# A token's two slots sorted by round, slot tables made with the rows as the stationary operand, and the last quad's second adds issued round by round

## The reference

```python
pg = softmax(t @ rg_w + rg_b);  pg_top, g_idx = top_k(pg, 1)        # one of 4 groups
le_sel = (t @ re_w + re_b).reshape(-1, 4, 4)[group of the token]
e_val, e_idx = top_k(le_sel, 2)                                     # two of its 4 experts
wts = softmax(e_val) * pg_top
y = hres + sum over the two experts of wts * ((silu(t @ w1) * (t @ w3)) @ w2)
```

## Time and profile before

| | us |
|---|---|
| median of 3 runs | 840.67 (837.34 to 842.12) |
| the profiled execution, its own time | 839.54 |
| its span in the trace | 837.7 |
| PE busy | 795.4 (95%) |
| DVE, ACT, POOL busy | 384.5, 225.9, 278.6 |

### The profile page before, as it was taken

One profiled execution on the slowest core, in us unless ns is written; L12 is line 12 of the kernel. 1 busy time (PEld: TensorE's weight loads), 2 busy tenths in 40 slices (PEclk: granted clock), 3 DMA queues, 4 the chain that ended last, 5 costly groups with the idle time before them and its releaser, 6 DMA issues.

```text
span 837.7 us, 14312 instructions
## 1 busy us (share of the span) xinstructions
PE 795.4 (95%) x5314; PEld 566.5 (68%) x5314; DVE 384.5 (46%) x700; ACT 225.9 (27%) x427; POOL 278.6 (33%) x204
## 2 busy tenths in 40 slices
PE   9999999989999998999999999999999789999991
PEld 8887777666677786777776777788888544333330
DVE  4671676757478589555551311543311632020210
ACT  4122324331423634114313222422201512020110
POOL 0000421244654773335453545523000021342223
PEclk9999999999999999999999999999999979999996
DMA  9243632245555531345453541161156769999943
GB/s 369 91 145 93 211 101 77 76 143 159 170 182 178 166 120 63 91 143 166 145 164 114 166 163 64 63 215 65 51 202 251 297 228 377 391 378 386 371 148 48
DMA packets 72154, 147.23 MB, mean 176 GB/s; under 512 B 13207, under 2 KB 47016, under 8 KB 70036
## 3 DMA queue, kind: packets, MB, share of 16 engines
q1 hardware_dynamic: 65716, 135.43, 46.0%
q0 software_dynamic: 5920, 10.82, 5.2%
q10 hardware_dynamic: 448, 0.06, 0.1%
HBM read 137.71 MB, written 18.90 MB: 187 GB/s over the span
## 4 chain that ended last, share of the span: by engine, by line
PE 85%; DVE 8%; ACT 2%; DMA 2%; issue 1%; POOLq 0%; POOL 0%; SPq 0%; DVEq 0%; ACTq 0%
PE ps L854 21%; PE ps L578 13%; PE ps L1157 10%; PE ps L1061 7%; PE ps L823 7%; PE ps L1226 5%; PE ps L621 3%; PE ps L593 3%; PE ps L876 2%; PE ps L923 2%; PE ps L653 2%; PE ps L567 1%; PE ps L1146 1%; DMA tmp<-in_xT 1%; PE ps L709 1%
## 5 line engine op out<-in xcount | busy, mean ns | idle before, releaser
L578 PE MATMUL ps<-xn,ring 128*128 128x268 f32 (+1 forms) x576 | 138.4, 395 | 1.0 <-ACT qb L1319 0.9
L578 PEld LDWEIGHTS ps<-xn,ring 128*128 128x128 f32 x576 | 108.2, 192 | 26.1 <-issue 3.4
L2415 POOL TENSOR_TENSOR kv<-kv,sgd 128x1024 f32<-128x1024 f32 (+1 forms) x32 | 79.9, 2510 | 120.0 <-DVE tmp L1760 70.3
L1462 ACT ACTIVATE sgt<-sgt,vec 128x260 f32<-128x260 f32 x60 | 30.2, 511 | 143.5 <-DVE sgt L2022 79.3
L823 PE MATMUL ps<-br,ring 128*128 128x260 f32 x256 | 61.7, 388 | 2.1 <-DVE sgt L2026 1.3
L2505 POOL DMA_INDIRECT out_y<-cst,gtab x24 | 37.3, 1555 | 76.4 <-DVE cst L2340 35.7
L854 PE MATMUL ps<-xn,ring 128*128 128x260 f32 x240 | 58.8, 388 | 2.3 <-ACT cst L1319 1.3
L854 PE MATMUL ps<-xn,qb 128*128 128x260 f32 x240 | 57.7, 383 | 0.0
L1061 PE MATMUL ps<-qk,ring 128*128 128x260 f32 x256 | 56.5, 383 | 0.0
L823 PEld LDWEIGHTS ps<-br,ring 128*128 128x128 f32 x256 | 47.6, 190 | 12.9 <-issue 2.8
L1061 PEld LDWEIGHTS ps<-qk,ring 128*128 128x128 f32 x256 | 48.6, 190 | 7.8 <-issue 0.4
(11 more groups left out here) (474 smaller groups left out, 1468.4 us busy)
## 6 DMA issues: line engine op xcount, KB each, us to landing
ring<-in_w_mg SPq DMA_DIRECT2D x32, 640.0 KB, 4.3
kv<-in_kc SPq DMA_DIRECT2D x128, 128.0 KB, 2.1
kv<-in_vc SPq DMA_DIRECT2D x128, 128.0 KB, 2.1
ring<-in_w_in SPq DMA_DIRECT2D x24, 512.0 KB, 4.7
kv<-in_w SPq DMA_DIRECT2D x8, 1024.0 KB, 15.0
br<-in_w SPq DMA_DIRECT2D x7, 1024.0 KB, 14.8
sgd<-in_w SPq DMA_DIRECT2D x6, 1024.0 KB, 16.4
qk<-in_w SPq DMA_DIRECT2D x6, 1024.0 KB, 12.2
```

What stands on the lines that cost most here:

```text
L578: mm = pe.matmul(ps[:, 2 * (t % 2) + h, 0:hw], wsl(c, k), xnv[:, k, col0 + h * hw:col0 + (h + 1) * hw], start=(k == 0), stop=(k == KT - 1))
L1462: act.activation(g, g, ACT.Sigmoid, bias=vv(V_BM + 8 * "ABCD".index(n) + m + i)).then_inc(g_a, 1)
L2415: pool.tensor_tensor(kb, kb, qbc[:, b:b + 1, :].to_broadcast([P, HALF // 2 + (half and u), 256]), ALU.mult)\
```

## The change

The positions of a token's two slots are sorted (`slot_f`: five minima, then five maxima), so kind 0 is the slot with the smaller position ("early") and kind 1 the other ("late"). The table matmuls have `oh_row` as the stationary operand and `marks` as the moving one, so that the result comes with slots on partitions and tiles on columns; it needs no transpose. Three are issued for each block: both kinds into one bank (the sum) and the late kind alone into another. The softmax weights are exchanged where the first choice is not the early one, and their table has two matmuls for each block. All `hTr` transposes are between the ranks and the table. `oh_row` of the first two blocks is made ahead of `marks`. In the last quad POOL issues the late adds of round r as soon as early adds of rounds up to r and late adds of the rounds before have landed.

```diff
-            rows_of(hTr, 0, NB)
 
             pe.wait_ge(sel_ok, 1)
...
-            for b in range(1, 3):
+            for b in range(NB):
                 rows_of(hTr, b, NB + b)
+
+            def by_rows(bk, j, b, mark, first, last):
+                return pe.matmul(ps[:, bk, 0:n_t], oh_row[0:RB, NB * j + b, :], marks[0:RB, mark, b, :], start=first, stop=last)
+
             for b in range(NB):
-                pe.wait_ge(oh_ok, 2 * b + 3)
+                pe.wait_ge(oh_ok, max(5, 2 * b + 3))
                 for j in range(2):
-                    mm = pe.matmul(ps[32 * j:32 * j + n_t, 5, 0:P], marks[0:RB, j, b, :], oh_row[0:RB, NB * j + b, :],
-                                   start=(b == 0), stop=(b == NB - 1), tile_position=(0, 32 * j))
+                    by_rows(4, j, b, j, b + j == 0, b + j == NB)
+                mm = by_rows(5, 1, b, 1, b == 0, b == NB - 1)
             mm.then_inc(tab_t[0], 1)
-            pe.wait_ge(sel_ok, 2)
-            pe.transpose(ps[:, 5, P:P + 64], slots[0:64], ident[0:64, 0:64]).then_inc(tab_tt[0], 1)
-            rows_of(hTr, 3, NB + 3)
-            rows_of(hTr, 4, NB + 4)
             pe.wait_ge(oh_ok, 2 * NB + 2)
-            pe.wait_ge(tt_a, NB + 3)
+            pe.wait_ge(tt_a, 2 * NB)
             for b in range(NB):
                 for j in range(2):
-                    mm = pe.matmul(ps[32 * j:32 * j + n_t, 2, 0:P], marks[0:RB, 2 + j, b, :], oh_row[0:RB, NB * j + b, :], ...
+                    mm = by_rows(7, j, b, 2 + j, b + j == 0, b + j == NB)
             mm.then_inc(wts_t[0], 1)
-            pe.wait_ge(sel_ok, 3)
-            pe.transpose(ps[:, 2, P:P + 64], slots[0:64], ident[0:64, 0:64]).then_inc(wts_tt[0], 1)
...
+                if i == 0:
+                    pe.wait_ge(g_ok, 1)
...
+            tt(slot_f[R, 0:NB], pos_f[R, 0:NB], pos_f[R, NB:2 * NB], ALU.min)
+            link(tt(slot_f[R, NB:2 * NB], pos_f[R, 0:NB], pos_f[R, NB:2 * NB], ALU.max))
...
             for b in range(NB):
+                if b == 2:
+                    dve.wait_ge(oh2_ok, 1)
+                    tt(marks[R, 0:2], oh_tile[R], tokid[R]...)\
+                        .then_inc(oh_ok, 1)
                 for n in range(2):
                     ts(oh_row[R, NB * n + b, :], io_row[R], row_f[R, ...], None, ALU.is_equal).then_inc(oh_ok, 1)
-            two_kinds(tab_t, 5)
-            dve.wait_ge(*tab_tt)
-            link(dve.tensor_copy(slots[:, 64:128], ps[:, 5, P:P + 64]))
-            link(tt(both, kinds[0], kinds[1], ALU.add))
+            dve.wait_ge(*tab_t)
+            both, second = ps[:, 4, 0:n_t], ps[:, 5, 0:n_t]
             link(ts(far, both, 0.0, float(FAR), ALU.is_equal, ALU.mult))
             stt(from_row[:, 0:n_t], both, -1.0, far, ALU.add, ALU.add).then_inc(tab_ok, 1)
+            link(dve.tensor_copy(late, second))
+            link(dve.memset(late[:, TILES:], 0.0))
+            link(tt(early, both, late, ALU.subtract))
...
+            tt(swap, pos_f[R, 0:NB].unsqueeze(2), pos_f[R, NB:2 * NB].unsqueeze(2), ALU.is_gt)
+            link(tt(diff, one[16], one[15], ALU.subtract))
+            link(tt(diff, diff, swap, ALU.mult))
+            tt(one[15], one[15], diff, ALU.add)
+            link(tt(one[16], one[16], diff, ALU.subtract))
             tt(marks[R, 2:4], oh_tile[R], rt[R, 15:17, :, 0:1]..., ALU.mult).then_inc(oh_ok, 1)
...
-            two_kinds(wts_t, 2)
-            dve.wait_ge(*wts_tt)
-            link(dve.tensor_copy(slots[:, 64:128], ps[:, 2, P:P + 64]))
-            tt(g_w[:, 0:n_t], kinds[0], kinds[1], ALU.add).then_inc(g_ok, 1)
+            dve.wait_ge(*wts_t)
+            dve.tensor_copy(g_w[:, 0:n_t], ps[:, 7, 0:n_t]).then_inc(g_ok, 1)
...
+            def second_choices(q, r):
+
+                for earlier in range(r + 1 if q == QUADS - 1 else ROUNDS):
+                    if r == 0 or q == QUADS - 1:
+                        pool.wait_ge(m_yst[earlier], 32 * q + (32 if earlier < r else 16))
+                add_rows(yb[r], to_row2[:, ROUNDS * q + r:ROUNDS * q + r + 1], m_yst[r])
...
                 first_choices(ROUNDS * q + 1)
+                if q == QUADS - 1:
+                    second_choices(q, 0)
                 first_choices(ROUNDS * q + 2)
-                second_choices(q)
+                if q == QUADS - 1:
+                    second_choices(q, 1)
+                    second_choices(q, 2)
+                    break
+                for r in range(ROUNDS):
+                    second_choices(q, r)
```

More of the change, by code:

```diff
@@ L257, in program @@
         g_w, slots = view(dr, 880, TILES + 2 * OVER), view(dr, 912, P)
-        row_f, tile_f, tokid = view(dr, 690, 10), view(dr, 700, 10), view(dr, 710, NB)
+        row_f, slot_f, tokid = view(dr, 690, 10), view(dr, 700, 10), view(dr, 710, NB)
         io_row, io_tile = view(dr, 720, P), view(dr, 720 + P, TILES + OVER + 1)
@@ L314, in program @@
         tt_t, tt_a, route_t = sem("tt_t"), sem("tt_a"), sem("route_t")
-        lgm, rank_ok, tab_t, tab_tt, wts_t, wts_tt = [(route_t, i + 1) for i in range(6)]
+        lgm, rank_ok, tab_t, wts_t = [(route_t, i + 1) for i in range(4)]
         rw_ok, lg_t, lg_a, lg_d = sem("rw_ok"), sem("lg_t"), sem("lg_a"), sem("lg_d")
@@ L1115, in _ @@
             pe.matmul(ps[:, 5, 0:NB * NE], every, selm, start=True, stop=True).then_inc(rank_ok[0], 1)
-            for b in range(1, 3):
+            for b in range(NB):
                 rows_of(hTr, b, NB + b)
+            def by_rows(bk, j, b, mark, first, last):
+                return pe.matmul(ps[:, bk, 0:n_t], oh_row[0:RB, NB * j + b, :], marks[0:RB, mark, b, :], start=first, stop=last)
             for b in range(NB):
-                pe.wait_ge(oh_ok, 2 * b + 3)
+                pe.wait_ge(oh_ok, max(5, 2 * b + 3))
                 for j in range(2):
-                    mm = pe.matmul(ps[32 * j:32 * j + n_t, 5, 0:P], marks[0:RB, j, b, :], oh_row[0:RB, NB * j + b, :],
-                                   start=(b == 0), stop=(b == NB - 1), tile_position=(0, 32 * j))
+                    by_rows(4, j, b, j, b + j == 0, b + j == NB)
+                mm = by_rows(5, 1, b, 1, b == 0, b == NB - 1)
             mm.then_inc(tab_t[0], 1)
-            pe.wait_ge(sel_ok, 2)
-            pe.transpose(ps[:, 5, P:P + 64], slots[0:64], ident[0:64, 0:64]).then_inc(tab_tt[0], 1)
-            rows_of(hTr, 3, NB + 3)
-            rows_of(hTr, 4, NB + 4)
             pe.wait_ge(oh_ok, 2 * NB + 2)
-            pe.wait_ge(tt_a, NB + 3)
+            pe.wait_ge(tt_a, 2 * NB)
             for b in range(NB):
                 for j in range(2):
-                    mm = pe.matmul(ps[32 * j:32 * j + n_t, 2, 0:P], marks[0:RB, 2 + j, b, :], oh_row[0:RB, NB * j + b, :],
-                                   start=(b == 0), stop=(b == NB - 1), tile_position=(0, 32 * j))
+                    mm = by_rows(7, j, b, 2 + j, b + j == 0, b + j == NB)
             mm.then_inc(wts_t[0], 1)
-            pe.wait_ge(sel_ok, 3)
-            pe.transpose(ps[:, 2, P:P + 64], slots[0:64], ident[0:64, 0:64]).then_inc(wts_tt[0], 1)
             def rows_T(u):
@@ L2274, in _ @@
             link(dve.tensor_reduce(pos_f[R, :], f12[R].rearrange("p n b g e -> p (n b) (g e)"), X, ALU.add))
-            tt(steps[R], pos_f[R, :].unsqueeze(2).to_broadcast([RB, 10, TILES + OVER + 1]),
+            tt(slot_f[R, 0:NB], pos_f[R, 0:NB], pos_f[R, NB:2 * NB], ALU.min)
+            link(tt(slot_f[R, NB:2 * NB], pos_f[R, 0:NB], pos_f[R, NB:2 * NB], ALU.max))
+            tt(steps[R], slot_f[R, :].unsqueeze(2).to_broadcast([RB, 10, TILES + OVER + 1]),
                io_tile[R].unsqueeze(1).to_broadcast([RB, 10, TILES + OVER + 1]), ALU.is_ge).then_inc(idx2_ok, 1)
@@ L2277, in _ @@
             dve.wait_ge(idx2_ok, 1)
[L2278 to L2281, removed]
+            link(dve.tensor_reduce(row_f[R, :], steps[R, :, 1:], X, ALU.add))
+            link(stt(row_f[R, :], row_f[R, :], -float(P), slot_f[R, :], ALU.mult, ALU.add))
@@ L2282, in _ @@
             for b in range(NB):
+                if b == 2:
+                    dve.wait_ge(oh2_ok, 1)
+                    tt(marks[R, 0:2], oh_tile[R], tokid[R].unsqueeze(1).unsqueeze(3).to_broadcast([RB, 2, NB, n_t]), ALU.mult)\
+                        .then_inc(oh_ok, 1)
                 for n in range(2):
                     ts(oh_row[R, NB * n + b, :], io_row[R], row_f[R, NB * n + b:NB * n + b + 1], None, ALU.is_equal).then_inc(oh_ok, 1)
-            def two_kinds(kind, bk):
-                dve.wait_ge(*kind)
-                dve.tensor_copy(slots[0:64, :], ps[0:64, bk, 0:P]).then_inc(sel_ok, 1)
@@ L2290, in _ @@
-            two_kinds(tab_t, 5)
-            dve.wait_ge(*tab_tt)
-            kinds = [slots[:, 64 + 32 * j:64 + 32 * j + n_t] for j in range(2)]
-            link(dve.tensor_copy(slots[:, 64:128], ps[:, 5, P:P + 64]))
-            both, far = io_row[:, 0:n_t], io_row[:, 32:32 + n_t]
-            link(tt(both, kinds[0], kinds[1], ALU.add))
+            far, far2, late, early = [io_row[:, 32 * k:32 * k + n_t] for k in range(4)]
```

(8 more changed lines are left out.)

## The result

| | before | changed |
|---|---|---|
| median, us | 839.64 (837.34 to 842.12, 4 executions) | 849.55 (847.37 to 852.08, 4) |
| span of the profiled execution, us | 837.7 | 847.4 |
| ratio | | 1.0106, 95% interval 1.0083 to 1.0129 |

The change makes the kernel 1.1% slower. The forecast was 842.1 and no change (838.4 to 845.4); 849.55 is outside that range. PE is busy for 801.3 us of the span, 95% as before. (The slices of the kernel before show PE under 9 tenths in five of the 40, not in two: three more stand at 8 tenths.)

What follows compares the result with a forecast made beforehand. PE, busy 95% of the span, was taken as the bound, so only routing and the end counted: 837.7 - 0.5 + 1.95 = 839.2 us span, 841.0 for that execution, median 842.1, range 838.4 to 845.4.

Steps and rivals of the forecast that it cites:

- The ranks start earlier: Routing: with the first hTr transposes gone from ahead, the ranks start 1.33 us earlier, all on the path.
- Five transpose groups hidden behind the ranks: Routing: groups of 1.0 to 1.1 us fill PE until about 666.5, at no cost, with 1.4 us of cover.
- The table matmuls: Routing, first table: 30 records take 3.2 us (2.6 to 3.8) instead of 20 records in 2.25.
- Reading it out: Routing, table to from_row: two instructions reading the accumulator take 0.5 us instead of 1.64; from_row at about 671.6.
- The weights' table: Routing, second table: 20 records in 2.1 us, hidden behind the gather with 1.0 us of cover.
- The clock: Routing and first layer: full-clock gain, half-clock loss and partly regained first-layer time taken together as a 0.5 us gain.
- rival 3: Routing: clock falls in the first table, weights' table outlasts the gather, first layer 2.7 us later; 845.3; chance 0.15.
- The end: Last quad's adds: three late adds each wait for a whole landing; span ends 1.95 us later.
- The upper end: Last quad's adds: with all landings at 5.5 us, late 2, the last late add, lands 839.1; loss 3.5.
- The sum: Whole kernel: 0.5 us gained in routing, 1.95 lost at the end; span 839.2 against 837.7.

Runs made afterwards that it cites:

- e7: Changed kernel plus two float32 matmuls of 512 columns, never read, in PE's wait ahead of the first table; ratio 1.0060 to the kernel before.
- e5: Changed kernel with tables made as before: marks stationary in two column groups, then copy, transpose, copy; ratio 1.0037 to the kernel before.
- e4: Changed kernel with the last two residual transpose groups behind the first table again; ratio 1.0114 to the kernel before.
- e6: Kernel before with first transposes behind the ranks, sorted slots, weight exchange, last-quad late adds waiting only for their round's early add; median 837.11 us, ratio 0.9945.
- e8: Kernel before with only the first residual transposes moved from ahead of the ranks to behind them; ratio 0.9988.
- e1: Changed kernel with the last quad's old add order: three early adds, wait for all to land, three late adds; ratio 1.0062 to the kernel before.
- e9: The kernel of e6 plus two unread float32 matmuls of 512 columns in PE's wait ahead of the first table; ratio 0.9971 to the kernel before.

## Why the prediction was wrong, step by step

- *The ranks start earlier*: right in place, 1.33 forecast. They start 0.30 us after the start of the DVE instructions that write `sel`, and DVE goes on at 661.96, after the 0.33 taken off 1.05 us earlier than 662.68.
- *Five transpose groups hidden behind the ranks*: right. They end at 666.2, the table starts at 668.42, 668.1 less the 0.33, against 667.9 forecast.
- *The table matmuls*, forecast 3.2 us (2.6 to 3.8): wrong as the central value, and the step that failed. The duration of a record was right at the high clock (0.107 forecast, 0.111 measured in e7), but the clock fell at 669.1, after six of the thirty, so they took 6.0. I had priced that case as a doubling of half the table, + 1.6; against e7's table it was + 2.5.
- *Reading it out*: 0.5 forecast; from 674.43 to 674.86 it is 0.43. `from_row` came at 674.86, 2.1 later than 672.41 when the 0.33 is taken off, not 0.8 earlier.
- *The weights' table*, forecast hidden: it was the last to end. It took 4.5 us and kept PE to 681.7, while the gather had landed at 680.4 (issued at 675.75, 4.6 to landing).
- *The clock*, for which I took a gain of 0.5 as a mean of good and bad cases: this was the reasoning at fault. I argued that PE, idle for 1.4 us instead of 4.2, would keep the clock at least as well; it was idle for 2.2, and the clock fell 0.7 us into the table. What rival 3 said happened instead: tables at half clock, the second behind the gather, transposes and first layer at half clock. (The section "HAM oscillation — how this bites in real kernels" that it names is in the Trainium skill's "TensorE: Matmul & The Clock Gate", not in the DMA page named just before it.) Its price was 2.7; routing lost 5.0. Missing were 1.2 by which the tables took still longer and the 1.1 of a first layer that stays at the low clock for 5.3 us. The chance of 0.15 was far too small, given that the trace of before already showed the fall in this place. Why the clock stayed low for 20.5 us stays open: with the old tables it was 13.7 (e5), and 10 us of busy PE didn't end it (e4).
- *The end*: right in mechanism, too small in size, 1.95 forecast, 4.3 measured. The mis-sized term is the landing: 5.5, 4.9, 5.1 and 3.8 us along the chain of waits, measured 6.0, 5.3, 6.1 and 4.5, 2.6 more together. I had worked them out by the number of rows alone, from adds of unsorted slots. Early 1, with 43 rows, landed after 5.9 us, and after 5.7 to 5.8 in e5, e6 and e7; unsorted, with 53 rows, it took 4.8 before and 5.0 in e8. The upper end was added wrongly, too: with every landing at 5.5 late 2 lands at 840.2 and not at 839.1, a loss of 4.65 and not 3.5, and the measured 4.3 is under it.
- *The sum*: + 1.5 forecast, + 9.7 in span. e5 puts 5 of it on tables and clock (4.3 in the front, 0.8 behind it), of which e7 shows 2.5 for the clock in the first table; e1 puts 3.6 on the waits between adds.

## What to carry to other kernels

Where one operand has 22 columns and the other 128, try the narrow one in the array: here 40 weight loads of 22 columns with a copy, a transpose and a copy behind them, seemingly wasted, were 5.8 us cheaper than 50 loads of 128 columns. When a stage's PE work is thin, price every instruction of it at the low clock, and ask first what the clock will be in the dense stage behind it. Keep only the waits that the data demands: adds to disjoint rows need no order, and the same reordering cost 4 us with the extra waits and gained 2 without. And before two traces are set side by side, bring them to a common start: e6's first layer looks 0.3 us late and is 0.6 early.

## What the runs showed that I had not expected

- PE busy for 4.00 of 4.00 us in two windows running, PEld for 4.00 and 3.97, and the granted clock at 0.50 throughout (e4).
- Two matmuls whose result nobody reads made a kernel 0.46% faster (e7). The same two in a better kernel went with 0.26% more (e9, barely clear of noise), where the low clock met the transposes and the first layer in place of the tables.
- An add of 43 rows landed in 5.9 us (changed kernel, early 1), where 53 rows took 4.8 before.
